# Packing the high and low parts of a 64-token tile into one stationary operand, in an fp32 encoder step on one TensorE

## The reference, cut to what matters

```python
def sgu_mixer(h, w_in, norm_g, w_s, b_s, w_out, rows):
    z = jax.nn.gelu(h @ w_in, approximate=False)          # h: tokens x 1024, w_in: 1024 x 4096
    u, v = jnp.split(z, 2, axis=-1)                       # v: tokens x 2048
    v = rms_norm(v, norm_g)
    ...
    mixed = jnp.einsum('gij,bcjgd->bcigd', ws, vg) + b_s
    y = u * mixed
    return y @ w_out, v
```

## Time and profile before

| | us |
|---|---|
| median of 3 runs | 1587.51 (1586.68 to 1588.81) |
| the profiled execution, its own time | 1590.08 |
| its span, first to last instruction | 1588.3 |
| TensorE matmuls busy in it | 1542.5 |
| GpSimd busy | 764.7 |
| VectorE busy | 613.1 |
| ScalarE busy | 382.3 |

### The profile page before, as it was taken

The page is one execution under the profiler, slowest core; times in us unless marked ns, Lnnn a source line. Parts: engine busy times, 40 slices in busy tenths (PEclk is TensorE's granted clock), DMA queues, the critical chain, the costliest instruction groups (busy, mean ns, idle before and its releaser), DMA issues.

```text
span 1588.3 us, 29034 instructions
## 1 busy us (share of the span) xinstructions
PE 1542.5 (97%) x10920; PEld 1460.2 (92%) x10920; DVE 613.1 (39%) x874; ACT 382.3 (24%) x875; POOL 764.7 (48%) x481
## 2 busy tenths in 40 slices
PE   6999999999999999999989999999999999999999
PEld 4778999999999999999976878787999999999998
DVE  6004726754314123134545455554454132141231
ACT  3323201122102011022237465665122011020110
POOL 6355454454555555555645052341355555555552
PEclk9999999999999999999999999998999999999999
DMA  7222232222222222222332010101122222222221
GB/s 233 67 69 77 66 116 79 66 80 80 81 80 80 82 90 80 79 79 83 125 94 71 1 54 1 53 13 40 42 78 81 88 84 80 79 80 87 84 78 48
DMA packets 36369, 120.16 MB, mean 76 GB/s; under 512 B 6040, under 2 KB 6744, under 8 KB 36064
## 3 DMA queue, kind: packets, MB, share of 16 engines
q1 hardware_dynamic: 30528, 110.25, 22.1%
q10 hardware_dynamic: 5792, 9.23, 1.9%
HBM read 115.91 MB, written 3.55 MB: 75 GB/s over the span
## 4 chain that ended last, share of the span: by engine, by line
PE 94%; DVE 2%; ACT 2%; issue 1%; DMA 0%; ACTq 0%; DVEq 0%
PE ps L539 28%; PE ps L541 27%; PE ps L540 27%; PE ps L868 2%; PE ps L847 2%; PE ps L803 1%; PE ps L637 1%; PE ps L876 1%; DVE neg_max L1222 1%; ACT kT L1487 1%; PE ps L806 1%; PE ps L817 1%; PE ps L788 1%; PE ps L744 1%; PE ps L706 0%
## 5 line engine op out<-in xcount | busy, mean ns | idle before, releaser
L484 POOL TENSOR_SCALAR w_hi<-raw 128x1024 fp32r<-128x1024 f32 x208 | 221.2, 1063 | 618.2 <-PE ps L541 615.2
L486 POOL TENSOR_TENSOR w_lo<-raw,w_hi 128x1024 fp32r<-128x1024 f32 x208 | 505.3, 2429 | 17.3
L539 PE MATMUL ps<-hid_hi,w_hi 128*128 128x288 f32 x1408 | 417.7, 297 | 2.1 <-DVE hid_lo L1146 2.1
L540 PE MATMUL ps<-hid_lo,w_hi 128*128 128x288 f32 x1408 | 416.0, 295 | 0.0
L541 PE MATMUL ps<-hid_hi,w_lo 128*128 128x288 f32 x1408 | 414.7, 295 | 0.0
L539 PE MATMUL ps<-h_hi,w_hi 128*128 128x288 f32 x1280 | 380.6, 297 | 0.0
L540 PE MATMUL ps<-h_lo,w_hi 128*128 128x288 f32 x1280 | 377.6, 295 | 0.0
L541 PE MATMUL ps<-h_hi,w_lo 128*128 128x288 f32 x1280 | 376.3, 294 | 0.0
L539 PEld LDWEIGHTS ps<-hid_hi,w_hi 128*128 128x128 f32 x1408 | 264.5, 188 | 2.3 <-issue 2.2
L541 PEld LDWEIGHTS ps<-hid_hi,w_lo 128*128 128x128 f32 x1408 | 265.8, 189 | 0.0
L540 PEld LDWEIGHTS ps<-hid_lo,w_hi 128*128 128x128 f32 x1408 | 265.0, 188 | 0.0
(11 more groups left out here) (155 smaller groups left out, 1664.3 us busy)
## 6 DMA issues: line engine op xcount, KB each, us to landing
raw<-stream SPq DMA_DIRECT2D x208, 512.0 KB, 3.5
out_x<-x ACTq DMA_DIRECT2D x8, 288.0 KB, 2.2
x<-xt ACTq DMA_DIRECT2D x4, 288.0 KB, 7.3
x<-xt SPq DMA_DIRECT2D x4, 288.0 KB, 8.2
b_bc<-bs ACTq DMA_DIRECT2D x2, 512.0 KB, 6.6
cache_raw<-cache_ct ACTq DMA_DIRECT2D x1, 1024.0 KB, 4.9
v_out<-sgu_grow ACTq DMA_DIRECT2D x1, 512.0 KB, 4.5
ws_sb<-ws ACTq DMA_DIRECT2D x2, 256.0 KB, 4.6
```

Of the source, the lines that this page charges most:

```text
L484: nc.gpsimd.tensor_scalar(w_hi[:, u, :], raw[:, u, :], 1.0, 0.0, ALU.mult, ALU.add).then_inc(split_hi, 1)
L486: nc.gpsimd.tensor_tensor(w_lo[:, u, :], raw[:, u, :], w_hi[:, u, :].bitcast(F32), ALU.subtract).then_inc(split_lo, 1)
L539: nc.tensor.matmul(out, l_hi, r_hi, start=first, stop=False)
L540: nc.tensor.matmul(out, l_hi, r_lo, start=False, stop=False)
```

## The change

It touches the 64-token tile of chunks 1, 2 and 3; chunk 0 stays as it was. A buffer `h_pair`, [128, 8, 128], holds for each k-slice the 64 columns of `h_hi` and beside them the 64 of `h_lo`. One matmul of `h_pair` with the high weights gives high x high in PSUM partitions 0 to 63 and low x high in partitions 64 to 127. A second one with 64 stationary columns adds high x low to partitions 0 to 63. After the chunk ScalarE copies partitions 64 to 127 into `mixed`, VectorE adds the other half and writes the sum into `v`, and ScalarE's Gelu then works in place on `v`. ScalarE's loop over the chunks is written out, with constant addresses.

```diff
+        h_pair = place("h_pair", [P, KD, 2 * DEC], F32R, b_at)
...
+            def packed(out, k, r_hi, r_lo, first, last):
+
+                nc.tensor.matmul(out, h_pair[:, k, :], r_hi, start=first, stop=False, skip_group_check=True)
+                return nc.tensor.matmul(out[0:DEC], h_hi[:, k, SEQ:T], r_lo, start=False, stop=last,
+                                        skip_group_check=True)
...
+                            if pack and t == NT - 1:
+                                last = packed(ps[:, bank_of(parity, t), 0:width], k, w_hi[:, j, w], w_lo[:, j, w],
+                                              k == 0, k == KD - 1)
+                                continue
...
+            pe.wait_ge(pair_set, 2)
             for c in range(1, 4):
-                token_chunk(c, c % 2, 4 * c, 512)
+                token_chunk(c, c % 2, 4 * c, 512, pack=True)
...
+            def fold_samples(n, out, bank):
+                width = out.shape[1]
+                dve.wait_ge(fold_set, n + 1)
+                nc.vector.tensor_tensor(out, ps[0:DEC, bank, 0:width], mixed[0:DEC, 0:width], ALU.add).then_inc(folded, 1)
...
             norm_diagonal(0)
+            for c in range(1, 4):
+                fold_samples(c - 1, v[0:DEC, NT - 1, c * 512:(c + 1) * 512], bank_of(c, NT - 1))
...
+            def copy_low_half(bank, width):
+                nc.scalar.copy(mixed[0:DEC, 0:width], ps[DEC:2 * DEC, bank, 0:width]).then_inc(fold_set, 1)
...
             load_half(0)
+            act.wait_ge(h_hi_set, KD)
+            nc.scalar.copy(h_pair[:, :, 0:DEC], h_hi[:, :, SEQ:T]).then_inc(pair_set, 1)
+            act.wait_ge(h_ready, KD)
+            nc.scalar.copy(h_pair[:, :, DEC:2 * DEC], h_lo[:, :, SEQ:T]).then_inc(pair_set, 1)
             norm_root(0)
             norm_take(0)
...
-            with act.Fori(0, 2, 1) as c2:
-                for parity in range(2):
...
+            for c in range(4):
+                parity = c % 2
...
+                    packed = c > 0 and t == NT - 1
+                    if packed:
+                        copy_low_half(bank_of(parity, t), 512)
+                        act.wait_ge(folded, c)
+                    nc.scalar.activation(vc, vc if packed else ps[0:r, bank_of(parity, t), :], ACT.Gelu,
+                                         scale=rms_tok[0:r, t:t + 1]).then_inc(tok_read, 1)
```

More of the change, by code:

```diff
@@ L301, in build_trunk @@
         tok_read = sem_of("tok_read")
+        pair_set = sem_of("pair_set")
+        fold_set = sem_of("fold_set")
+        folded = sem_of("folded")
         v_set = sem_of("v_set")
@@ L579, in norm_spread, with token_chunk @@
                 last.then_inc(rms_spread, 1)
-            def token_chunk(chunk, parity, first_unit, width, between=None, h_count=None, tiles=None):
+            def packed(out, k, r_hi, r_lo, first, last):
+                nc.tensor.matmul(out, h_pair[:, k, :], r_hi, start=first, stop=False, skip_group_check=True)
+                return nc.tensor.matmul(out[0:DEC], h_hi[:, k, SEQ:T], r_lo, start=False, stop=last,
+                                        skip_group_check=True)
+            def token_chunk(chunk, parity, first_unit, width, between=None, h_count=None, tiles=None, pack=False):
                 for j in range(4):
@@ L1318, in _ @@
             act.wait_ge(set_up, SETUPS)
-            with act.Fori(0, 2, 1) as c2:
-                for parity in range(2):
[L1321 to L1333, removed]
+            for c in range(4):
+                parity = c % 2
+                for t in range(NT):
+                    r = ROWS[t]
+                    if t < NT - 1:
+                        act.wait_ge(tok_done, c * 4 + (t + 1))
+                    else:
+                        act.wait_ge(unit_done, c * 4 + 4)
+                    vc = v[0:r, t, c * 512:(c + 1) * 512]
+                    packed = c > 0 and t == NT - 1
[4 more added lines that the diff above has]
+                                         scale=rms_tok[0:r, t:t + 1]).then_inc(tok_read, 1)
+                    act.wait_ge(tok_read, c * 5 + (10 + t + 1))
+                    nc.scalar.activation(junk[0:r, :], vc, ACT.Square,
+                                         accum_out=ss_v[0:r, t, c:c + 1]).then_inc(ss_v_set, 1)
             act.wait_ge(rms_v_step, 3)
```

## The result

The changed kernel took 1578.82 us (median of 7 executions, 1577.04 to 1583.37), the kernel before 1589.05 (7 executions, three of them those shown above). The ratio is 0.9936, 95% interval 0.9922 to 0.9951. The forecast stood on three executions whose median, 1587.51, was low: the median of the 148 executions measured later is 1589.77. Against that one the forecast ratio gives 1584.2, and the miss is larger than the first numbers say.

A forecast was written before the change was run, and what follows sets the result against it. TensorE, fully busy in the chunk stretch, was taken as the bound. Terms -5.46 - 0.27 + 0.1 = -5.6 us took the median from 1587.51 to 1581.9 us, ratio 0.9965, range 1579.8 to 1584.7.

The forecast's parts named there:

- What was removed: 64-token tile, chunks 1 to 3: 24 fewer TensorE matmuls at 0.2273 us each, 5.46 us saved.
- The 3.1 us estimated from the Trainium skill's figure: Alternative saving for the 24 matmuls at about 131 ns each; the prediction set it aside for the trace's 227 ns.
- rival (d): Packed matmuls in chunks 1 to 3 save less than a whole matmul, half of 5.46 us goes: 1584.6 us; chance 0.05.
- What was added before chunk 1 and in each chunk: Two ScalarE pair copies before chunk 1, then a copy and VectorE add per chunk: hidden, cost nothing for chunks 1 and 2.
- The written-out loop: ScalarE in chunk 0: three Gelu-to-Square gaps each 0.09 us shorter, so TensorE's stall in chunk 1 shrinks by 0.27 us.
- The tail up to the `vn` products: Behind chunk 3: TensorE waits for the norm of v before its first `vn` product, 0.1 us added.
- (b): Behind chunk 3: GpSimd's `w_lo` holds VectorE's add, TensorE waits and a half-clock stretch follows: 1585.2 us; chance 0.06.
- (c): Behind chunk 3: a later tail puts `vn` behind the next `w_lo`, TensorE waits 4.4 us: 1587.8 us; chance 0.03.
- Rival (a): Chunk 1: the shorter stall may not bring the half-clock stretch, which costs 1.6 us: 1580.3 us; chance 0.12.
- the rest is moved, not changed: After the `vn` products TensorE's order of work and waits stay as they were; no term in the sum.
- S: Theory formed after the result: mean clock depends on when the attention stage is reached; about 0.990 with 24 matmuls out.

The follow-up runs named there:

- the cut one: Kernel before, ended behind the first MLP, without attention and second MLP: 782.80 us; the changed kernel with the same cut: 777.52 us.
- without the low product: Kernel before with ScalarE's loop written out and low x high of the 64-token tile left out in chunks 1 to 3, no packing: ratio 0.9951.
- chunk 0 in a loop of one: Changed kernel with ScalarE's work on chunk 0 put back in a hardware loop of one turn: ratio 0.9934.
- longer stall: Changed kernel with one more ScalarE pass ahead of the Gelu of chunk 0's tile 3: ratio 0.9946.
- Two further kernels: Changed kernel with chunk 3 not packed, ratio 0.9975; changed kernel with chunk 1's tiles reordered so TensorE need not stall, ratio 0.9949.

## Why the prediction was wrong

**What was removed: right.** 24 matmuls, 0.2273 expected for each; 0.2273 in the packed units' period and in chunk 3 alone, 0.232 with them put back. The 3.1 us estimated from the Trainium skill's figure are out (TensorE: Matmul & The Clock Gate, section Back-to-back issue gap: 131 ns for a matmul of 512 columns in a stream; 227 here). Half-width matmuls cost a full one, so rival (d) is out too.

**What was added before chunk 1 and in each chunk: right.** The two pair copies took 0.62 and 0.61 us (0.59 expected) and were hidden, though they began at 33.76 and not at 30.9. The last piece of `h_hi` began 2.8 us later in this trace (28.44 against 25.62), as it does in the second trace of the kernel before (28.95). The table load behind the copies ended at 36.20 and the square root began at 38.83, so the cover was 2.6 us and not 6. The fold took 0.68 (0.69), the copy 0.58 (0.59). The kernel with the matmuls put back shows them free.

**The written-out loop: right in the trace** (stall 1.89, 1.86 and then 1.58; 0.27 expected), too small for the totals.

**The tail up to the `vn` products: right.** A wait of 0.12 us, 0.1 expected; the scale was free of GpSimd, and rivals (b) and (c) did not come up: the add beside `w_lo` took 0.68.

**Rival (a), the clock in chunk 1**, had the right mechanism and too firm a reading. In the first pair of traces it occurred just as priced, 1.6 us. But of four traces with this stall (three of the whole kernel before, one of the cut one, 1.86 to 1.89 us) one has the half clock, and a stall of 2.10 had none. Behind the shorter stalls of 1.58 to 1.61 us none of thirteen traces has it. It is an event of some executions; one in four of 1.6 us would be 0.4 us in the mean, an estimate from four traces.

**The step that failed is the last of the tail: "the rest is moved, not changed".** Its order of work is the same, but TensorE's clock in the attention stage is not. From chunk 1's start to chunk 3's end two traces of the same clock differ by 84.12 - 78.43 = 5.69 us (5.46 + 0.27 = 5.73 expected), the cut kernels by 5.3. The whole kernels differ by 7.7 ± 0.75 us in the mean and by 9.8 in the median, since the changed kernel's times bunch low with a long tail (1576.6 to 1601.9). The mean clocks are 0.9877 and 0.9896: of the span that is 19.5 and 16.4 us lost, a difference of 3.1. 5.3 + 3.1 = 8.4 is within the error of 7.7. The single traces behind chunk 3 (1451.5 to 1462.1 us, the same code) show where it lies. The sum had no term for it, and the range, built from single mechanisms ahead of the attention, no room for it. The profile before did hold a warning that I used only for its size: a mean clock of 0.989, which is 17 us of the span, and one half-clock stretch near the change, which is 1.6 of them. Most of the loss had to be elsewhere. The three executions, 2.1 us apart, also looked steadier than the kernel is: the later 148 lie between 1583.7 and 1596.2.

**What decides the clock there** is narrowed, not settled. The four kernels that reach the attention stage 5 to 6 us early (changed, without the low product, chunk 0 in a loop of one, longer stall) have 0.9896 ± 0.0004 over 78 executions, the three that reach it within 0.3 us of the old time 0.9877 ± 0.0002 over 184. What the four share is the time taken out, not the packing. That speaks for S, though 51 of the 78 are of the changed kernel itself and the grouping was made afterwards. Two further kernels, 4 and 8 us early, have 0.9885 ± 0.0006 and 0.9888 ± 0.0007; they lie between the groups, within two of their own errors of either, so whether earlier is better step by step stays open. Why 5.7 us should be a good amount, no run here shows; a pure delay of several lengths ahead of the attention stage was not tried.

**A better version.** The changed kernel without the stall takes 2.1 us less in the cut form (775.42 against 777.52) and its mean in full is 1580.2 ± 1.0 against 1582.1 ± 0.7. It beats the kernel before (0.9949, 0.9929 to 0.9969); that it beats the changed kernel is shown only in the cut form.

## What to carry to other kernels

Price a removed matmul by the distance between starts in its own stage, with its own width of stationary operand: here half-full columns cost as much as full ones, so two halves side by side win a whole matmul, and fold and copies are free where ScalarE and VectorE have a chunk's time for them. Before giving a narrow range, look where the kernel loses clock: a stage that stands far behind the change can answer a shift of a few microseconds with half as much again (3.1 us on 5.3 here), and single executions differ there by 10. To measure a change of a few microseconds in such a kernel, cut it off ahead of the stage that spreads, or compare the starts of two events around the change in single traces.

## What the runs showed of the hardware

With 5.7 us taken out ahead of it, a stage 670 us later lost less granted clock: the mean over the whole launch went from 0.9877 to 0.9896, worth 3 us, and putting the matmuls back undid it with all the rest of the edit in place. A second edit that takes out as much gave 0.9892 ± 0.0010, which points the same way and proves little alone. Executions of kernels with different edits share the same few places where the clock falls: where these agree, the time behind the change did too (1454.5 and 1454.4 us; 1452.4, 1452.3 and 1452.1; 1462.1 and 1461.2).

A matmul with 64 stationary columns took 0.230 us from start to start, one with 128 took 0.227. In ScalarE's loop the register operation for an address lengthened the gap between Gelu and Square from 0.03 to 0.12 us; the one ahead of the next Gelu ran beside the Square (at 50.25 in the first trace) and cost nothing. A stall that a trace shows as 1.58 us of idle cost TensorE 1.84 us between starts.
